# Plain fp32 value matmuls, to-and-fro triples and a packed copy of h in a two-layer encoder step

## The chip, the cores and the metric
The kernel runs on one core of a Trainium2 chip. The time is device microseconds of one execution of the whole program. Five engines work from queues of their own and meet at semaphores: TensorE (PE; its weight loads are shown as PEld), VectorE (DVE), ScalarE (ACT), GpSimd (POOL) and SyncE (SP), which issues most of the DMA transfers.

## What is computed
One inference step of a two-layer encoder on a prompt of 1024 rows and eight samples of 16 rows, 1024 features wide, all in float32. Layer 0 runs differential attention (A, 4 heads of 128) and grouped attention over a sliding window (B, 8 query heads of 64) side by side; layer 1 runs chunk-band attention with a bias by relative position (C, 16 heads of 64). Each attention is followed by a gated feed-forward block with a causal convolution of width 3. Every sub-layer starts with a modulated RMSNorm.

```python
def diff_core(q, k, v, lam, mask):            # A
    s = jnp.einsum('bqhcd,bkhcd->bhcqk', q, k).astype(jnp.float32) * ATTN_SCALE
    p = jax.nn.softmax(jnp.where(mask, s, NEG_INF), axis=-1)
    w = p[:, :, 0] - lam * p[:, :, 1]
    return jnp.einsum('bhqk,bkhe->bqhe', w.astype(v.dtype), v)
...
def relbias_core(q, k, v, table, qpos, kpos, mask):      # C; B likewise, with sinks
    s = jnp.einsum('bqhd,bkhd->bhqk', q, k).astype(jnp.float32) * ATTN_SCALE + bias
    p = jax.nn.softmax(jnp.where(mask, s, NEG_INF), axis=-1)
    o = jnp.einsum('bhqk,bkhd->bqhd', p.astype(v.dtype), v)
...
def conv_ffn(h, conv_state, w_up, conv_w, conv_b, w_down):
    u = h @ w_up
    up = jnp.concatenate([conv_state, u], axis=1)
    y = conv_b
    for j in range(CONV_W):
        y = y + up[:, j:j + t] * conv_w[j]
    a, g = jnp.split(y, 2, axis=-1)
    return (jax.nn.silu(g) * a) @ w_down, up[:, -(CONV_W - 1):]
```

## The kernel before
The program is a chain of stages: setup, attention A and B with the out-projection of layer 0, feed-forward 0, attention C with its out-projection, feed-forward 1, and the final norm. Features stand on the partitions; a row block of the activation h is 128 features by 1152 columns (1024 of the prompt and 8 x 16 of the samples), and there are 8 of them (k = 0 to 7).

Float32 products are made from parts. A value is kept as a high part (type fp32r, which TensorE takes in one pass) and a low part in bf16 (h and hl, w and wl). mm3 (L84) makes one product from a triple of matmuls: high weights by high values (L86), the upper two bytes of the high weights by the low values (L87), and the low weights by the upper two bytes of the high values (L88). The upper two bytes are read in place by `top` (L79), every second two-byte element. pair3 (L114) is the same triple for the values of B and C, with v as the weights and 256 columns of softmax weights (two heads) as the moving operand. mm9 (L90) makes three triples at a time for one weight block of the feed-forward, with the columns of h in pieces of 512, 512 and 128, and puts the three fp32r matmuls (L96) next to each other; L98 is upper weights by hl, L100 low weights by the upper half of h.

Attention goes over tiles: four A tiles (T = 0 to 3), four B tiles, eight C tiles. A tile has eight units u of 128 queries and two stream units for the samples. The steps of a tile are laid out by hand in tile_steps (L1278), and every engine walks through the same list. For unit u the softmax weights E are transposed by TensorE (step T, L1940, L1945, L1950), ACT copies them from PSUM to W as fp32r (L2201), and VectorE subtracts W from the same PSUM bank to get the bf16 low part Wl (L2339). Step V (L1955 on) waits for that subtraction (semaphore w_low) and multiplies W, Wl with v, vl, one triple per block of 128 keys: as many blocks as the unit sees, u + 1 in A, min(u + 1, 2) in B, min(u + 1, 5) in C. v itself is copied by ACT (L2180) and its low part vl made by VectorE (L2328), both in step VS. A stream unit's values (step PV, L1980) are already done in plain fp32 from Ws, in four column tiles of 32. Ws shares its memory with Wl.

Between these steps the planner places the projections as fill: steps F make q, k and v of the next tile, and at the end steps P make the first 6 of 8 parts of the out-projection. Each of them is one mm3 for one k and one third (384) of the columns, and the steps of one third follow each other in the order of k, with the tile's own steps in between. They have due places in the list; a third whose last k is done is evacuated by ACT.

In the feed-forward, first_pair (L896) multiplies the first two up tiles while the norm is still being made, one k at a time: VectorE scales (L628), ACT writes the high part of h (L598, semaphore hp_high), VectorE the low part (L633). The other 42 up tiles run up_tile (L918) with one mm9 per k. GpSimd only loads the convolution state (L845) and makes small copies (L872, L873) in this stage.

Of the kernel before, what the change touches and what calls it, by code (L numbers as in the profile page):

```python
# [8 lines left out]
F32 = mybir.dt.float32  # L9
# [5 lines left out]
P = 128  # L15
# [74 lines left out]
def mm9(pe, ps, acc, w, wl, x, xl, start, stop):  # L90

    def one(b, which, first, last):
# [7 lines left out]
        return pe.matmul(out, wl, top(x[:, lo:hi]), start=first and start, stop=last and stop, skip_group_check=True)  # L100
# [13 lines left out]
def pair3(pe, out, v, vl, w, wl, start, stop):  # L114

    pe.matmul(out, v, w, start=start, stop=False, skip_group_check=True)
    pe.matmul(out, top(v), wl, start=False, stop=False, skip_group_check=True)
    return pe.matmul(out, vl, w.bitcast(BF16)[:, :, 1::2], start=False, stop=stop, skip_group_check=True)
# [585 lines left out]
def ffn(nc, S, G, ins, outs, l):  # L704
    ctx = ExitStack()
    with ctx:
# [19 lines left out]
        ring.own[fb + FCH - 1] = sb("w_z", [P, D], F32R), sb("wl_z", [P, D], BF16)  # L726
        if l == 0:
# [114 lines left out]
        def _(pool):  # L842
# [16 lines left out]
            earlier(0)  # L859

# [31 lines left out]
        def _(pe):  # L892
# [86 lines left out]
            def body(i):  # L979
# [9 lines left out]
                else:  # L989
                    first_pair(c)  # L990
                c += 1
# [385 lines left out]
def attention(nc, S, G, ins, outs, kinds):  # L1377
    ctx = ExitStack()
    with ctx:
# [19 lines left out]
        Ws = Wl[:, :].bitcast(F32)  # L1399
# [438 lines left out]
        def _(pe):  # L1838
# [3 lines left out]
            def do(what, kind, T, s, c, turns):  # L1842
                n = kv(kind, T)
                first = isinstance(T, int) and T == T0
                if what == "F":
# [10 lines left out]
                    mm = mm3(pe, ps[:, f_bank(T, name, b), 0:hi - lo], w[:, k * P:(k + 1) * P], wl[:, k * P:(k + 1) * P],  # L1856
                             h[:, k, lo:hi], hl[:, k, lo:hi], k == 0, k == KT - 1)
# [23 lines left out]
                elif what == "P":  # L1881
# [12 lines left out]
                    mm = mm3(pe, ps[:, i % 2, 0:hi - lo], w[:, k * P:(k + 1) * P], wl[:, k * P:(k + 1) * P],  # L1894
                             h[:, k, lo:hi], hl[:, k, lo:hi], k == 0, k == KT - 3)
# [56 lines left out]
                elif what == "V" and s[1] < QB:  # L1952
# [8 lines left out]
                    for j in range(nb):  # L1961
                        x, y = slice(j * P, (j + 1) * P), slice((k0 + j) * P, (k0 + j + 1) * P)
                        if kind == "A":
                            mm = mm3(pe, ps[:, 7, 0:P], W[:, x], Wl[:, x], v[:, y], vl[:, y], j == 0, j == nb - 1)
                        else:
                            both, low = (t[:, 0:2 * nb * P].rearrange("p (z x) -> p z x", z=2)[:, :, x] for t in (W, Wl))
                            mm = pair3(pe, pair_o(kind, u).rearrange("p (z x) -> p z x", z=2), v[:, y], vl[:, y], both, low,
# [141 lines left out]
        def _(act):  # L2109
# [17 lines left out]
            def do(what, kind, T, s, c, turns):  # L2127
# [49 lines left out]
                elif what == "VS":  # L2177
                    act.wait_ge(S.v_rows, n + 1)
                    act.copy(vn[:, :], sw[:, SEQ:TOK])
                    act.copy(v[:, :], sw[:, :]).then_inc(S.v_high, 1)  # L2180
# [12 lines left out]
                elif what == "T":  # L2193
# [100 lines left out]
        def _(dve):  # L2294
# [16 lines left out]
            def do(what, kind, T, s, c, turns):  # L2311
# [14 lines left out]
                elif what == "VS":  # L2326
                    dve.wait_ge(S.v_high, n + 1)
                    dve.tensor_tensor(vl[:, :], sw[:, :], v[:, :].bitcast(F32), ALU.subtract).then_inc(S.v_low, 1)  # L2328
# [4 lines left out]
                elif what == "T":  # L2333
                    u, p = s[1:]
                    if u >= QB:
                        return
# [357 lines left out]
```

## Time and profile before

| | us |
|---|---|
| median of 3 runs | 3491.92 (3490.02 to 3502.86) |
| the profiled execution | 3502.18 |
| its span on the core | 3500.6 |
| TensorE busy | 3215.5 (92%) |
| VectorE busy | 1853.9 (53%) |
| ACT busy | 1195.0 (34%) |
| GpSimd busy | 428.0 (12%) |

Read the busy time of each engine by stage first, then, for the engine that is busy nearly all the time, what ended its waits, and last single stretches in order of time. Times in the rows are microseconds from the start of the span, unless marked ns.
### The profile page before, as it was taken

How to read it: one execution, taken by the hardware profiler on the slowest of the kernel's cores; microseconds unless marked ns; L12 is line 12 of the kernel's file. 1: busy time of each engine (PE TensorE's matmuls, PEld its weight loads, DVE VectorE, ACT ScalarE, POOL GpSimd, SP SyncE). 2: the span in 40 equal slices, each digit the busy share in tenths (PEclk: the TensorE clock that was granted, in tenths of full speed). 3: DMA queues.
4: the chain of work that ended last, by engine and by line, in shares of the span. 5: the costliest groups of instructions: out<-in, count | busy, mean ns of one | idle time of the engine just before them, and what ended most of it. 6: DMA issues, size and time to landing. Idle time of an engine off the chain costs nothing. (4 is left out here: it accounts for less than half of the span.)

```text
span 3500.6 us, 53118 instructions
## 1 busy us (share of the span) xinstructions
PE 3215.5 (92%) x20564; PEld 2019.7 (58%) x20758; DVE 1853.9 (53%) x3222; ACT 1195.0 (34%) x2527; POOL 428.0 (12%) x820
## 2 busy tenths in 40 slices
PE   7888896888899999999979999998989999999998
PEld 3455553445566666666545555555555666666665
DVE  4355554554655545554555555554636555555546
ACT  3355554533321222222235555554433122222121
POOL 1132222311000000000002222221110000000000
PEclk7899997989999999999999999999999999999998
DMA  9233332231422222222123443444421111111111
GB/s 355 79 105 106 86 90 61 77 115 34 123 62 67 67 66 61 61 79 87 50 84 110 134 133 126 135 135 153 132 64 46 43 49 43 43 43 38 43 43 61
DMA packets 247845, 305.16 MB, mean 87 GB/s; under 512 B 25027, under 2 KB 199607, under 8 KB 247042
## 3 DMA queue, kind: packets, MB, share of 16 engines
q1 hardware_dynamic: 217762, 191.78, 17.5%
q0 software_dynamic: 29920, 111.15, 10.5%
q8 instruction: 109, 1.79, 0.2%
q14 instruction: 54, 0.44, 0.0%
HBM read 265.99 MB, written 64.10 MB: 94 GB/s over the span
## 5 line engine op out<-in xcount | busy, mean ns | idle before, releaser
L96 PE MATMUL psum<-h,ffn_high 128*128 128x512 f32 (+1 forms) x2016 | 587.0, 399 | 2.8 <-ACT u L1069 2.8
L98 PE MATMUL psum<-hl,ffn_high 128*128 128x512 bf16 (+1 forms) x2016 | 553.3, 328 | 0.0
L96 PEld LDWEIGHTS psum<-h,ffn_high 128*128 128x128 f32 x2016 | 377.9, 188 | 134.7 <-issue 8.4
L100 PE MATMUL psum<-h,ffn_low 128*128 128x512 bf16 (+1 forms) x1901 | 444.1, 328 | 7.4
L86 PE MATMUL psum<-h,attC_high 128*128 128x384 f32 (+2 forms) x768 | 361.6, 471 | 23.9 <-issue 8.3
L1142 DVE TENSOR_SCALAR y<-u,cvT 128x1168 f32<-128x1168 f32 x88 | 78.1, 888 | 521.2 <-ACT u L1074 521.0
L86 PE MATMUL psum<-h,attAB_high 128*128 128x384 f32 (+2 forms) x672 | 326.2, 486 | 18.3 <-DVE attAB_low L189 8.5
L98 PEld LDWEIGHTS psum<-hl,ffn_high 128*128 128x128 bf16 x2016 | 194.9, 97 | 244.7
L96 PE MATMUL psum<-actr,ffn_high 128*128 128x512 f32 (+1 forms) x960 | 277.5, 397 | 7.5 <-DVE xT L672 7.5
L98 PE MATMUL psum<-actl,ffn_high 128*128 128x512 bf16 (+1 forms) x960 | 265.0, 330 | 0.0
L1068 ACT COPY u<-psum 128x1024 f32<-128x1024 f32 x88 | 89.3, 1015 | 511.5 <-PE psum L98 511.1
L87 PE MATMUL psum<-hl,attC_high 128*128 128x384 bf16 (+2 forms) x766 | 262.1, 342 | 0.0
L88 PE MATMUL psum<-h,attC_low 128*128 128x384 bf16 (+2 forms) x767 | 258.9, 338 | 0.3 <-issue 0.2
L87 PE MATMUL psum<-hl,attAB_high 128*128 128x384 bf16 (+2 forms) x670 | 235.7, 352 | 0.0
L88 PE MATMUL psum<-h,attAB_low 128*128 128x384 bf16 (+2 forms) x671 | 232.6, 347 | 0.3 <-issue 0.2
L672 DVE SCALAR_TENSOR_TENSOR xT<-psum,mod,xT 128x1024 f32<-128x1024 f32 x176 | 224.8, 1277 | 0.0
L96 PEld LDWEIGHTS psum<-actr,ffn_high 128*128 128x128 f32 x960 | 178.2, 190 | 70.4 <-DVE xT L672 16.5
L100 PE MATMUL psum<-actr,ffn_low 128*128 128x512 bf16 (+1 forms) x900 | 212.9, 330 | 3.8
L872 POOL COPY so<-u 128x2 f32<-128x2 f32 x88 | 17.8, 202 | 1520.2 <-ACT u L1069 1520.2
L86 PEld LDWEIGHTS psum<-h,attC_high 128*128 128x128 f32 x768 | 149.6, 195 | 84.0 <-issue 39.6
L86 PEld LDWEIGHTS psum<-h,attAB_high 128*128 128x128 f32 x672 | 136.4, 203 | 66.4 <-issue 29.9
L183 ACT CAST ffn_high<-ffn_raw 128x1024 fp32r<-128x1024 f32 x42 | 44.2, 1053 | 372.6 <-PE psum L98 372.6
(470 smaller groups left out, 5921.4 us busy)
## 6 DMA issues: line engine op xcount, KB each, us to landing
raws<-in_w_up SPq DMA_DIRECT2D x66, 512.0 KB, 3.9
ada_raw<-in_ada_w SPq DMA_DIRECT2D x24, 1024.0 KB, 9.4
m_raw<-in_ada_w SPq DMA_DIRECT2D x48, 512.0 KB, 7.5
raw_C<-in_cache_c_v POOLq DMA_DIRECT2D x64, 256.0 KB, 4.0
out_ck_s<-in_cache_c_k POOLq DMA_DIRECT2D x8, 1984.0 KB, 8.9
out_cv_s<-in_cache_c_v POOLq DMA_DIRECT2D x8, 1984.0 KB, 15.0
raws<-in_w_in_odd SPq DMA_DIRECT2D x24, 512.0 KB, 12.5
raw_C<-in_cache_c_k POOLq DMA_DIRECT2D x48, 256.0 KB, 5.6
```

Of the source, the lines that this page charges most:

```text
L86: pe.matmul(out, w, x, start=start, stop=False, skip_group_check=True)
L87: pe.matmul(out, top(w), xl, start=False, stop=False, skip_group_check=True)
L88: return pe.matmul(out, wl, top(x), start=False, stop=stop, skip_group_check=True)
L96: return pe.matmul(out, w, x[:, lo:hi], start=first and start, stop=last and stop, skip_group_check=True)
L98: return pe.matmul(out, top(w), xl[:, lo:hi], start=first and start, stop=last and stop, skip_group_check=True)
L100: return pe.matmul(out, wl, top(x[:, lo:hi]), start=first and start, stop=last and stop, skip_group_check=True)
L183: act.copy(self.buffers(c)[0][:, :], self.raw[c % self.raws][:, :]).then_inc(self.high[s], 1)
L672: return dve.scalar_tensor_tensor(out=G.xT[:, n, 0:SEQ], in0=y[:, 0:SEQ], scalar=G.mod[:, a, 16 + n, 0:1], in1=G.xT[:, n, 0:SEQ], op0=ALU. ...
L872: pool.tensor_copy(so[:, 2 * g + j, 0:2], U[g][:, SEQ:SEQ + 2])
L1068: act.copy(U[gate][:, 2:2 + SEQ], ps[:, 3 * gate:3 * gate + 2, :].rearrange("p b n -> p (b n)"))
L1142: ch.then(dve.tensor_scalar(y[:, 0:n], u[:, 2:2 + n], cv[:, l, 2, bass.ds(f, 1)], cv[:, l, 3, bass.ds(f, 1)], ALU.mult, ALU.add))
```

## The change
There are three parts.

1. Values (steps T, V and VS). W and v become plain fp32 tiles. The low parts Wl and vl, VectorE's subtractions for them and the semaphores of the high parts are gone; ACT's copies now release TensorE directly (w_low, v_low). pair3 and the triple of A give way to `plain`: four fp32 matmuls on 32 columns of the weights each, into 32 partitions of the output each. Ws gets memory of its own.
2. Projections (steps F and P). Odd k run their triple in reverse order, so that the fp32r matmul of an odd k is the last of its triple and that of the next even k the first of its own.
3. Feed-forward 1 only. GpSimd copies h to a packed bf16 tile hb, one copy of 128 x 1024 after each hp_high and one of 128 x (8 x 128) for the samples after hs_high, ahead of its other work in the stage. The 42 up tiles read hb in place of the upper half of h (L100). TensorE waits for all nine copies after first_pair.

```diff
+def mm3_to_and_fro(pe, out, w, wl, x, xl, k, stop):
+
+    if k % 2 == 0:
+        return mm3(pe, out, w, wl, x, xl, k == 0, stop)
+    pe.matmul(out, wl, top(x), start=False, stop=False, skip_group_check=True)
+    pe.matmul(out, top(w), xl, start=False, stop=False, skip_group_check=True)
+    return pe.matmul(out, w, x, start=False, stop=stop, skip_group_check=True)
+
+
-def mm9(pe, ps, acc, w, wl, x, xl, start, stop):
+def mm9(pe, ps, acc, w, wl, x, xl, start, stop, xb=None):
...
-        return pe.matmul(out, wl, top(x[:, lo:hi]), start=first and start, stop=last and stop, skip_group_check=True)
+        whole = top(x[:, lo:hi]) if xb is None else xb[:, lo:hi]
+        return pe.matmul(out, wl, whole, start=first and start, stop=last and stop, skip_group_check=True)
...
-def pair3(pe, out, v, vl, w, wl, start, stop):
-
-    pe.matmul(out, v, w, start=start, stop=False, skip_group_check=True)
-    pe.matmul(out, top(v), wl, start=False, stop=False, skip_group_check=True)
-    return pe.matmul(out, vl, w.bitcast(BF16)[:, :, 1::2], start=False, stop=stop, skip_group_check=True)
+def plain(pe, out, w, x, start, stop):
+
+    for j in range(4):
+        cols = slice(32 * j, 32 * j + 32)
+        mm = pe.matmul(out[cols], w[:, cols], x, start=start, stop=stop, skip_group_check=True)
+    return mm
...
+        hb = sb("hb", [P, KT, TOK], BF16) if l else None
...
+            if l:
+                for k in range(KT):
+                    pool.wait_ge(S.hp_high, KT * m + k + 1)
+                    settle(pool, S)
+                    pool.tensor_copy(hb[:, k, 0:SEQ], h[:, k, 0:SEQ].bitcast(F32)).then_inc(S.h_short, 1)
+                pool.wait_ge(S.hs_high, m + 1)
+                settle(pool, S)
+                pool.tensor_copy(hb[:, :, SEQ:TOK], h[:, :, SEQ:TOK].bitcast(F32)).then_inc(S.h_short, 1)
...
-                             h[:, k, :], hl[:, k, :], k == 0, k == KT - 1)
+                             h[:, k, :], hl[:, k, :], k == 0, k == KT - 1, hb[:, k, :] if l else None)
...
                     first_pair(c)
+                    if l:
+                        pe.wait_ge(S.h_short, KT + 1)
...
-        v, vl = sb("v", [P, TOK], F32R), sb("vl", [P, TOK], BF16)
+        v = sb("v", [P, TOK])
...
-        W, Wl = sb("W", [P, 1280], F32R), sb("Wl", [P, 1280], BF16)
+        W, Ws = sb("W", [P, 1280]), sb("Ws", [P, 640])
...
-                            mm = mm3(pe, ps[:, 7, 0:P], W[:, x], Wl[:, x], v[:, y], vl[:, y], j == 0, j == nb - 1)
+                            mm = plain(pe, ps[:, 7, 0:P], W[:, x], v[:, y], j == 0, j == nb - 1)
...
-                    if u < QB:
-                        act.copy(W[:, cols], src).then_inc(S.w_high, 1)
-                    else:
-                        act.copy(Ws[:, cols], src).then_inc(S.w_low, 1)
+                    act.copy((W if u < QB else Ws)[:, cols], src).then_inc(S.w_low, 1)
...
-                elif what == "VS":
-                    dve.wait_ge(S.v_high, n + 1)
-                    dve.tensor_tensor(vl[:, :], sw[:, :], v[:, :].bitcast(F32), ALU.subtract).then_inc(S.v_low, 1)
...
-                    dve.wait_ge(S.w_high, t_no(kind, T, u, p) - 2 * T)
-                    cols, src = probs_at(kind, T, u, p)
-                    dve.tensor_tensor(Wl[:, cols], src, W[:, cols].bitcast(F32), ALU.subtract).then_inc(S.w_low, 1)
```

## Rows read from the trace of the kernel before

**Rows 1.** Stages C and feed-forward 1: stretch, length, busy by engine, clock, DMA share, GB/s

```profile
1764.00:2663.00 899.00, 798.70 (x5740) 504.52 (x5744) 457.81 (x1004) 408.68 (x903) 163.65 (x252) 0.97 0.38 119
2663.00:3472.00 809.00, 798.36 (x4635) 513.75 (x4720) 455.94 (x527) 189.37 (x293) 34.38 (x120) 1.00 0.13 40
```

**Rows 2.** What TensorE waited for, 1831 to 2545 (C): total, times, longest us

```profile
PE psum L116 <- DVE Wl_C L2339: 27.8, 24, 2.3
...
PE psum L1950 <- DVE Wl_C L2339: 7.9, 16, 1.6
```

**Rows 3.** What TensorE waited for, 533 to 832 (B tiles)

```profile
PE psum L1945 <- DVE E_AB L2460: 14.3, 4, 8.4
PE psum L116 <- DVE Wl_AB L2339: 13.6, 15, 1.9
```

**Rows 4.** What TensorE waited for, 93 to 533 (A tiles)

```profile
PE psum L86 <- DVE actl_AB L2351: 8.8, 13, 2.2
```

**Rows 5.** TensorE in order of time, value triples of C: start, us, operation

```profile
2050.85 0.36 PE L116 MATMUL psum<-W_C,v_C 128*128 128x256 f32 x1
...
2051.91 0.36 PE L116 MATMUL psum<-W_C,v_C 128*128 128x256 f32 x1
```

**Rows 6.** TensorE in order of time, a run of column tiles (stream values of C)

```profile
2075.57 0.33 PE L88 MATMUL psum<-h,attC_low 128*128 128x384 bf16 x1
2075.83 1.08 PE L1980 MATMUL psum<-raw_C,Wl_C 128*32 128x128 f32 x32
2076.73 0.40 PE L1980 MATMUL psum<-vn_C,Wl_C 128*32 128x128 f32 x8
...
2077.35 0.34 PE L87 MATMUL psum<-hl,attC_high 128*128 128x384 bf16 x1
```

**Rows 7.** TensorE in order of time, value triples of A

```profile
364.37 0.30 PE L86 MATMUL psum<-v_AB,W_AB 128*128 128x128 f32 x1
...
364.86 0.31 PE L86 MATMUL psum<-v_AB,W_AB 128*128 128x128 f32 x1
```

**Rows 8.** TensorE in order of time, projection triples: the first and the fifth

```profile
2012.17 0.48 PE L86 MATMUL psum<-h,attC_high 128*128 128x384 f32 x1
...
2014.27 0.48 PE L86 MATMUL psum<-h,attC_high 128*128 128x384 f32 x1
```

**Rows 9.** TensorE in order of time, value units that wait: [idle before <-releaser]

```profile
2057.14 0.39 PE L116 MATMUL psum<-W_C,v_C 128*128 128x256 f32 x1 [1.25 <-DVE Wl_C L2339]
...
2062.58 0.38 PE L116 MATMUL psum<-W_C,v_C 128*128 128x256 f32 x1 [1.05 <-DVE Wl_C L2339]
```

**Rows 10.** ACT in order of time, the copy that belongs to the first of them

```profile
2054.88 0.37 ACT L2201 CAST W_C<-psum 128x256 fp32r<-128x256 f32 x1 [0.41 <-PE psum L1950]
```

**Rows 11.** VectorE by line and shape, 1764 to 2663: busy us, mean ns, idle before

```profile
L2339 DVE TENSOR_TENSOR Wl_C<-psum,W_C 128x512 bf16<-128x512 f32 x96 | 62.7, 687 | 115.3 <-ACT W_C L2201 115.3
```

**Rows 12.** TensorE in order of time, two steps of mm9

```profile
2900.02 0.59 PE L98 MATMUL psum<-hl,ffn_high 128*128 128x512 bf16 x2
...
2901.56 0.59 PE L98 MATMUL psum<-hl,ffn_high 128*128 128x512 bf16 x2
```

**Rows 13.** TensorE by line and shape, 2703 to 3440 (feed-forward 1)

```profile
L98 PE MATMUL psum<-hl,ffn_high 128*128 128x512 bf16 x624 | 184.8, 377 | 0.0
L100 PE MATMUL psum<-h,ffn_low 128*128 128x512 bf16 x575 | 179.8, 386 | 3.1
```

**Rows 14.** GpSimd by line and shape, the whole span

```profile
L1668 POOL MEMSET bt_C<- 128x768 f32 x1 | 0.7, 746 | 0.0
```

**Rows 15.** ACT in order of time, the last row block of h

```profile
2651.70 1.15 ACT L598 ACTIVATE h<-u,mod 128x1024 fp32r<-128x1024 f32 x1 [1.36 <-DVE u L628]
```

**Rows 16.** GpSimd and VectorE in order of time, the same microsecond

```profile
2665.26 0.79 POOL L873 COPY so<-u 128x16 f32<-128x16 f32 x1
...
2665.11 0.89 DVE L1142 TENSOR_SCALAR y<-u,cvT 128x1168 f32<-128x1168 f32 x1 [9.81 <-ACT u L1074]
```

**Rows 17.** TensorE in order of time, in first_pair

```profile
2645.38 0.49 PE L86 MATMUL psum<-h,ffn_high 128*128 128x512 f32 x1 [0.45 <-DVE hl L633]
```

More of the change, by code:

```diff
@@ L1398, in attention @@
         Qs, kn, vn = sb("Qs", [P, P]), sb("kn", [P, P]), sb("vn", [P, P])
-        Ws = Wl[:, :].bitcast(F32)
         early = [E[:, e:e + 512].rearrange("p (j d) -> p j d", d=P) for e in ((640, 1920) if odd else (1280,))]
@@ L1855, in do @@
                     lo, hi = THIRDS[b]
-                    mm = mm3(pe, ps[:, f_bank(T, name, b), 0:hi - lo], w[:, k * P:(k + 1) * P], wl[:, k * P:(k + 1) * P],
-                             h[:, k, lo:hi], hl[:, k, lo:hi], k == 0, k == KT - 1)
+                    mm = mm3_to_and_fro(pe, ps[:, f_bank(T, name, b), 0:hi - lo], w[:, k * P:(k + 1) * P],
+                                        wl[:, k * P:(k + 1) * P], h[:, k, lo:hi], hl[:, k, lo:hi], k, k == KT - 1)
                     if k == KT - 1:
@@ L1893, in do @@
                     lo, hi = THIRDS[b]
-                    mm = mm3(pe, ps[:, i % 2, 0:hi - lo], w[:, k * P:(k + 1) * P], wl[:, k * P:(k + 1) * P],
-                             h[:, k, lo:hi], hl[:, k, lo:hi], k == 0, k == KT - 3)
+                    mm = mm3_to_and_fro(pe, ps[:, i % 2, 0:hi - lo], w[:, k * P:(k + 1) * P], wl[:, k * P:(k + 1) * P],
+                                        h[:, k, lo:hi], hl[:, k, lo:hi], k, k == KT - 3)
                     if k == KT - 3:
@@ L1963, in do @@
                         if kind == "A":
-                            mm = mm3(pe, ps[:, 7, 0:P], W[:, x], Wl[:, x], v[:, y], vl[:, y], j == 0, j == nb - 1)
+                            mm = plain(pe, ps[:, 7, 0:P], W[:, x], v[:, y], j == 0, j == nb - 1)
                         else:
-                            both, low = (t[:, 0:2 * nb * P].rearrange("p (z x) -> p z x", z=2)[:, :, x] for t in (W, Wl))
-                            mm = pair3(pe, pair_o(kind, u).rearrange("p (z x) -> p z x", z=2), v[:, y], vl[:, y], both, low,
+                            both = W[:, 0:2 * nb * P].rearrange("p (z x) -> p z x", z=2)[:, :, x]
+                            mm = plain(pe, pair_o(kind, u).rearrange("p (z x) -> p z x", z=2), v[:, y], both,
                                        j == 0, j == nb - 1)
@@ L2179, in do @@
                     act.copy(vn[:, :], sw[:, SEQ:TOK])
-                    act.copy(v[:, :], sw[:, :]).then_inc(S.v_high, 1)
+                    act.copy(v[:, :], sw[:, :]).then_inc(S.v_low, 1)
                 elif what == "KR":
@@ L2332, in do @@
                     maxima(kind, T, s[1], 0, stream_width(kind))
[L2333 to L2336, printed above, removed]
-                    dve.wait_ge(S.w_high, t_no(kind, T, u, p) - 2 * T)
-                    cols, src = probs_at(kind, T, u, p)
-                    dve.tensor_tensor(Wl[:, cols], src, W[:, cols].bitcast(F32), ALU.subtract).then_inc(S.w_low, 1)
                 elif what == "FA":
@@ L2586, in __init__ @@
             "rope_in dup_in qz_zero q_evac k_evac v_evac q_high q_low")
-        (self.k_high, self.k_low, self.v_high, self.v_low, self.v_rows, self.k_rows, self.v_turned, self.k_turned) = make(
-            "k_high k_low v_high v_low v_rows k_rows v_turned k_turned")
+        (self.k_high, self.k_low, self.h_short, self.v_low, self.v_rows, self.k_rows, self.v_turned, self.k_turned) = make(
+            "k_high k_low h_short v_low v_rows k_rows v_turned k_turned")
         (self.stored,) = make(
@@ L2594, in __init__ @@
             "qz scores stream_scores nmax exps probs turned")
-        (self.w_high, self.w_low, self.pv, self.od, self.od_turned, self.squares, self.ms, self.rstd) = make(
-            "w_high w_low pv od od_turned squares ms rstd")
+        (self.w_low, self.pv, self.od, self.od_turned, self.squares, self.ms, self.rstd) = make(
+            "w_low pv od od_turned squares ms rstd")
         (self.o_rows, self.o_turned, self.act_high, self.act_low, self.out_ready, self.out_evac) = make(
```

## The prediction

> **What bounds the kernel now.** The first view to read is the busy time of the engines by stage. In the second feed-forward stage TensorE is busy 798 of 809 us, in attention C 799 of 899 [rows 1]; VectorE is about half busy in both. So in the feed-forward stage a nanosecond taken from a matmul is a nanosecond of the time, while attention C holds some 100 us in which TensorE stands still. The second view says for what: in the steady part of C its largest entry is the low part of the softmax weights, Wl, which VectorE makes at L2339: 27.8 us in 24 waits ahead of the value matmuls and 7.9 in 16 ahead of the next transposes [rows 2]. In the B tiles the same subtraction costs 13.6 us and other work of VectorE 14.3 [rows 3]. In the A tiles no wait names it, but 8.8 us go to actl (L2351), another VectorE step that queues behind it [rows 4]. The change takes that subtraction away and pays with TensorE time, so the two must be set against each other; the two other parts are small and certain by comparison.
>
> **Plain values, the cost.** Per tile and per value unit u (8 per tile, 16 tiles, 128 units) the code runs one block per 128 keys. By the loops these are 1+2+...+8 = 36 blocks per A tile, 1+7x2 = 15 per B tile, 1+2+3+4+5x4 = 30 per C tile.
> A block of B or C is now a triple over 256 columns: four of them take 2050.85 to 2051.91, less the first, so three steps are 1.06, 0.353 each [rows 5]. After it is four 32-column fp32 matmuls. The trace has this form already in the stream values, L1980: 40 records in one run, which are 5 blocks, 4 column tiles, 2 passes [rows 6]. The first 32 records (8 passes over 128 columns) start 0.90 ahead of the last 8, so a pass of the four tiles is 0.1125 at most and two are 0.225; four cycles a column at the granted 2.4 GHz would be 0.213. I take 0.22 for 128 columns and 0.43 for 256. A block of B or C so costs 0.077 more. A block of A is now 0.245 (two from 364.37 to 364.86 [rows 7]) and becomes 0.025 cheaper.
> There is also an edge. Around that run L88 starts at 2075.57 and the next L87 at 2077.35: 1.78. Without it L88 to L87 is 0.36 (a step of 0.525 [rows 8] less one bf16 matmul of 384 columns, 0.16 at 2.4 GHz). Less ten passes (1.10) this leaves 0.32 for entering and leaving the column tiling. That is paid for each of the 128 units, as the triples of before have no edge of that kind.
> Sum: C 8 x (30 x 0.077 + 8 x 0.32) = 39.0; B 4 x (15 x 0.077 + 2.56) = 14.9; A 4 x (2.56 - 36 x 0.025) = 6.6. In all +60.5 us of TensorE time. Bounds: if the exit (a weight load of the next triple, some two thirds of the edge) is hidden, 60 - 27 = 33; with 0.225 and 0.45 per block 68.
>
> **Plain values, the relief.** The release of a unit becomes the end of ACT's copy of W. At 2057.14 TensorE had waited 1.25 for Wl [rows 9], since 2055.89; ACT's copy of that piece had ended at 2055.25 [rows 10]. That wait goes altogether. What is late next is the last unit of a tile, as at 2062.58 (1.05) [rows 9], where I leave 0.47 because ACT's copy itself comes late; the same allowance for the waits at the stage's end leaves 30 of 35.7 us. A wait also costs more than its idle time: from L88's end in the run of matmuls to the first value matmul the pipeline refills, 0.1 to 0.27 us, I take 0.17: 40 x 0.17 = 7. C gains 37 (bounds 20, if 0.7, the length of one subtraction [rows 11], goes from each of the 24 and half of the 16 stays, to 43).
> In B the subtraction follows ACT's copy directly and is 0.7 long [rows 11], so of the 13.6 two thirds go, 9; and VectorE, quit of it, serves its other waits (14.3) earlier: 5 more. B gains 14 (5 to 18). In A the subtraction stands ahead of actl: of 8.8 I take 6, and 3 for the maxima and factors behind it: 9 (0 to 12). The subtractions for vl lie under the projections and are worth nothing. Sum of the relief 60, so plain values net +60.5 - 60 = **+0.5 us**.
>
> **Reversed triples.** A step of four triples of 384 columns is 2.10 from 2012.17 to 2014.27, 0.525 each [rows 8]; 1152 columns at 2.4 GHz are 0.480, so 45 ns go to overhead, in which is one change to fp32 weights and back. A step of mm9 does three times the columns with one such change: 1.540 [rows 12], 100 ns over 1.440. If s is the price of the change and t what goes with the columns, s + t = 45 and s + 3t = 100: t = 27, s = 18. Turned odd k put the fp32 matmul of odd k beside that of k + 1 where the planner leaves the two adjacent, which, counted in the planner's order of steps, is 368 times in 1344 triples (most runs between other steps are two long). 368 x 18 = 6.6 us at most; as the second fp32 weight load has only 0.16 us of matmul to hide under, I take 0.0145: **-5.3**. Bounds: 0.03 lost each time, +11, and -13 if the odd step's end beside fp32 transposes also counts.
>
> **The two-byte copy of h.** L100 reads the upper half of h in place: 386 ns against 377 for L98, which reads packed hl with the same columns [rows 13]; 9 ns. 42 up tiles x 8 k x 2 pieces of 512 x 9 ns = **-6.0** (bounds 0 to -9), all on the path, since this stage is TensorE. The copies: a GpSimd memset of 768 columns is 0.746 [rows 14], so 1024 columns are 1.0 us by estimate, nine of them. The wait on h_short stands behind first_pair. The last h is written by ACT at 2652.85 [rows 15]; copies queued behind it end by some 2656, and TensorE gets there at 2663: 7 us of cover, nothing behind it on TensorE's queue is late. If the copies were three times as long they would still end in time. On GpSimd's own queue only the first state rows (due 2665) stand behind them. But each copy starts on the same event as VectorE's low(k), L633. In the trace a GpSimd copy of 128x16 that is otherwise 0.2 to 0.3 us lasts 0.79 and ends with VectorE's L1142 beside it [rows 16]: the two hold each other up. TensorE waits for low(3) at 2645.38 (0.45 idle) [rows 17], and has growing slack after it. I take **+1.5** (bounds 0 and +4.2).
> The Trainium skill says of this pair of engines (SBUF — State Buffer, section "SBUF: two separate sides") that they share a port pair as an exclusive lock for a whole instruction, and that a VectorE operation with two SBUF inputs takes it against a GpSimd operation that reads SBUF. The trace agrees as far as [rows 16] goes; by that rule every one of the eight low(k) could lose a whole copy, about 8 us by estimate, of which the slack takes half.
>
> **Sum.** +0.5 - 5.3 - 6.0 + 1.5 = -9.3. The profiled execution took 3502.18 (span 3500.6 and 1.6 around it) and would take 3492.9. It was 10.3 above the median of the runs, 3491.92; on the median the forecast is 3482.6, said as 3483. What a measurement of this kernel can tell from no change is about 0.5%, 17.5 us.
>
> **Rivals.**
> Slow: the relief doesn't come. ACT's copies are late too: ACT waits for the transposes (0.41 ahead of its copy [rows 10]) and runs the evacuations in between, so TensorE, arriving at the same place, stops on the copy. With the low bounds C gains 20, B 5, A 0: 25 in place of 60, and the time is 3483 + 35 = 3518. It turns slower than 0.5% when less than 33 of the 60 comes back. Against it: in the row looked at the copy ended 0.6 us ahead of TensorE's need.
> Fast: the edge is mostly hidden. The triple that follows a unit begins with a bf16 weight load where k is odd, and the exit, two thirds of 0.32, is that load; half of the units gain 0.2: -13. VectorE, quit of the subtractions, also takes half of what is left of B's 14.3 and A's waits, and pipeline refills at 0.27: -12. That gives 3458.
> Small parts fail: the strided read is no cost of its own, and the 9 ns come from the place behind fp32 or a weight load (+6); the merged fp32 loads aren't covered, so no gain and a few lost (+8); VectorE is held (+3). Then 3500. The Trainium skill gives a reason for the first (SBUF — State Buffer, the box on cachelines under "Door 1: The DMA port swizzle"): two-byte elements may be strided free as long as two hits fall in a 16-byte line, which every second element does. By it the copy would bring 0 instead of -6.0; the rows show 386 against 377.
> The change doesn't do what it says: if the four column tiles ran one after the other, a block would cost four times 0.43; the 40 records in 1.8 us [rows 6] exclude that.
>
> **How the numbers follow.** Forecast (sum between -25 and +8, own range 3467 to 3500) 0.48, fast 0.20, small parts fail 0.20, slow 0.12. The range runs from 3457 to 3508: it leaves out most of the slow case and less than half of the fast one. Faster by over 0.5% (under 3474.5): the fast case and a fifth of the forecast, 0.30. Slower (above 3509.4): slow case and a little of the third, 0.13. The rest, 0.57, within 0.5%.
>
> **What would show it.** Right: in C no wait on L2339's place longer than 0.6 us but the last unit's, TensorE's busy time in C up by 35 to 45 us at about equal length of the stage; L1980-like runs with 0.32 around them; L86 twice in a row with a step of two triples near 1.03; L100 at L98's 377; first_pair longer by under 4. Wrong: TensorE waits on L2201 in the same number as before on L2339, an edge of 0.1 or of 0.5, or L100 unchanged.

## The result, and the profile after

The changed kernel takes 3457.96 us (median of 4 runs, 3450.08 to 3461.78) beside 3495.13 for the kernel before (median of 4): a ratio of 0.9889 with a 95% interval of 0.9861 to 0.9917. Measured again beside eleven more runs of before it was 0.9876 (0.9861 to 0.9890). So it is faster by 37 to 43 us. The forecast was 3483, a gain of 9.3: the sign was right, and the size a quarter of what came. The time lies a microsecond inside the lower end of the stated range (3457 to 3508), and beside the 3458 of the fast rival, for reasons that neither had.

First the busy time of the engines by stage. The columns are the stretch, its length, busy time and instructions of TensorE, its weight loads, VectorE, ACT and GpSimd, then the granted clock of TensorE, DMA share and GB/s. The four stretches are the A tiles, the B tiles with the out-projection, attention C, and feed-forward 1 from the first up tile on. Kernel before:

```profile
97.40:520.29 422.89, 376.53 (x2757) 240.54 (x2761) 215.46 (x524) 208.05 (x522) 112.26 (x183) 0.95 0.33 94
520.29:889.32 369.03, 289.39 (x1893) 168.88 (x1888) 189.88 (x517) 148.89 (x445) 73.03 (x115) 0.89 0.25 74
1779.77:2633.52 853.75, 763.12 (x5562) 485.61 (x5565) 426.38 (x978) 393.65 (x887) 158.37 (x242) 0.98 0.39 121
2665.03:3494.58 829.55, 815.48 (x4732) 529.11 (x4818) 467.77 (x538) 189.44 (x292) 34.38 (x120) 0.99 0.14 43
```

The same four of the changed kernel:

```profile
94.86:505.02 410.16, 360.98 (x3477) 236.93 (x3481) 187.37 (x472) 207.92 (x522) 112.85 (x183) 0.97 0.34 97
505.02:865.89 360.87, 290.71 (x2195) 166.95 (x2188) 169.09 (x483) 149.29 (x445) 72.52 (x115) 0.90 0.25 75
1755.39:2589.18 833.79, 769.70 (x6765) 477.51 (x6765) 339.58 (x826) 395.35 (x887) 159.62 (x243) 0.99 0.39 124
2621.54:3442.46 820.92, 813.17 (x4818) 530.96 (x4818) 467.77 (x538) 189.51 (x292) 34.94 (x120) 0.99 0.14 43
```

A is 12.7 us shorter, B and its out-projection 8.2, C 20.0, feed-forward 1 8.6. (These two executions are 52 us apart, more than the medians: the one of before was among the longest of its kernel, the one of the changed kernel the shortest.) In C, TensorE is busy 6.6 us longer in a stage 20 us shorter, where the prediction's sign of being right was 35 to 45 us longer at about equal length. And in the three attention stretches the granted clock is a hundredth or two higher. A hundredth of a stretch of 400 us is 4 us, so that column can't be passed over; the experiments below come back to it.

Next what TensorE waited for in steady C of the changed kernel (total, times, longest us):

```profile
PE psum L1966 <- DVE E_C L2468: 10.0, 13, 1.1
...
PE psum L128 <- DVE actl_C L2364: 5.9, 8, 1.1
...
PE psum L1971 <- ACT W_C L2221: 2.0, 3, 1.3
...
PE psum L128 <- ACT W_C L2221: 1.0, 2, 0.5
```

The 35.7 us of [rows 2] are gone. What is late next is not ACT's copy (3.0 in all) but actl, one per tile, 5.9: the last unit of a tile, which the forecast had left at 0.47 for ACT's copy and which waits 0.6 to 1.1 for another step.

One plain value unit of four blocks, TensorE in order of time, with plain values alone:

```profile
2019.78 0.33 PE L88 MATMUL psum<-h,attC_low 128*128 128x384 bf16 x1
2020.04 1.93 PE L124 MATMUL psum<-W_C,v_C 128*32 128x256 f32 x32
2021.91 0.55 PE L1956 MATMUL psum<-consts,E_C 128*128 128x128 f32 x3
```

and the same unit in the kernel before, first and last of its rows:

```profile
2035.17 0.33 PE L88 MATMUL psum<-h,attC_low 128*128 128x384 bf16 x1
...
2036.77 0.49 PE L1950 MATMUL psum<-consts,E_C 128*128 128x128 f32 x3
```

From L88 to the transposes it was 1.60 and is 2.13: 0.53 dearer, where the forecast had 4 x 0.077 + 0.32 = 0.63 with an exit that partly falls behind the transposes. The prices of [rows 5, 6] carry over: in the trace of plain values with the subtraction still waited for (below), units of C that don't wait are dearer by 0.30, 0.38, 0.45, 0.53 and 0.61 with one to five blocks, which is 0.077 a block, as forecast, and an edge of 0.22 before what falls behind.

### The profile page after: what moved, and what is told of

It is laid out like the page before. It is cut to its first block and busy times, and to the rows that moved or that the text cites. A ratio compares the mean times of both kernels' runs of the same rounds, so it can differ in the third digit from the quotient of the medians.

```text
span 3448.5 us, 57532 instructions
## 1 busy us (share of the span) xinstructions
PE 3210.5 (93%) x22978; PEld 2005.8 (58%) x22978; DVE 1719.6 (50%) x2984; ACT 1197.2 (35%) x2527; POOL 442.6 (13%) x829
## 3 DMA queue, kind: packets, MB, share of 16 engines
q8 instruction: 126, 2.06, 0.3%
## 5 line engine op out<-in xcount | busy, mean ns | idle before, releaser
L110 PE MATMUL psum<-h,ffn_low 128*128 128x512 bf16 (+1 forms) x1008 | 225.8, 332 | 0.0
L110 PE MATMUL psum<-hb,ffn_low 128*128 128x512 bf16 (+1 forms) x1008 | 219.5, 327 | 0.0
L86 PE MATMUL psum<-h,attC_high 128*128 128x384 f32 (+2 forms) x408 | 159.7, 394 | 21.3 <-issue 8.3
L96 PE MATMUL psum<-h,attC_high 128*128 128x384 f32 x360 | 170.1, 473 | 0.0
L86 PE MATMUL psum<-h,attAB_high 128*128 128x384 f32 (+2 forms) x360 | 148.1, 412 | 17.8 <-DVE attAB_low L200 8.5
L107 PEld LDWEIGHTS psum<-actl,ffn_high 128*128 128x128 bf16 x960 | 93.2, 97 | 117.4 <-issue 2.5
L96 PE MATMUL psum<-h,attAB_high 128*128 128x384 f32 x312 | 150.5, 482 | 0.0
L87 PE MATMUL psum<-hl,attC_high 128*128 128x384 bf16 (+2 forms) x408 | 138.8, 340 | 0.0
L88 PE MATMUL psum<-h,attC_low 128*128 128x384 bf16 (+2 forms) x408 | 136.7, 335 | 0.0
```

Source lines behind the costliest of these rows:

```text
L86: pe.matmul(out, w, x, start=start, stop=False, skip_group_check=True)
L87: pe.matmul(out, top(w), xl, start=False, stop=False, skip_group_check=True)
L88: return pe.matmul(out, wl, top(x), start=False, stop=stop, skip_group_check=True)
L96: return pe.matmul(out, w, x, start=False, stop=stop, skip_group_check=True)
L107: return pe.matmul(out, top(w), xl[:, lo:hi], start=first and start, stop=last and stop, skip_group_check=True)
L110: return pe.matmul(out, wl, whole, start=first and start, stop=last and stop, skip_group_check=True)
```

## The experiments

All times stand beside runs of the kernel before on the same chip. Besides the ratio I read one more number from the runs. Each run lists its span and its mean granted clock; the clock has two levels in these traces, 1.0 (2.4 GHz) and 0.5. Span times clock is the time the span would have at full clock, and the rest is lost to stretches at the half clock (an upper bound, since a TensorE that stands loses nothing; but in the profiles TensorE is at half clock for 250 us before and 198 after, and busy for 197 and 149 of these, so nearly all of the fall is time in which it works). Before: 3372 and 122 us, the mean of 23 runs. Differences are to before, with two standard errors; the clock is listed to a thousandth.

### Plain values alone
The edit leaves out the other two parts:

```diff
-    if k % 2 == 0:
-        return mm3(pe, out, w, wl, x, xl, k == 0, stop)
...
+    return mm3(pe, out, w, wl, x, xl, k == 0, stop)
...
-                    if l:
-                        pe.wait_ge(S.h_short, KT + 1)
```

> Plain fp32 values alone; the triples of the projections all forward, the low-weight matmuls of feed-forward 1 read h in place. Theory W (what the change gains is TensorE's standing still for Wl, and the half-clock stretches that go with it): 20 to 30 us below the kernel before, two thirds of the gain of the whole change, in attention AB and C alike, with fewer microseconds at the granted clock 0.5 in both. Rival R (the gain is the reversed triples): within 6 us of before. The forecast's sum said +0.5.

3477.44 beside 3495.44, ratio 0.9939 (0.9922 to 0.9955), spans shorter by 18.8 in the mean. At full clock that is only -4.5 ± 1.6; -14.3 ± 4.1 is less time lost to the half clock. So plain values alone give about half of the gain, a little under the 20 to 30 us and two thirds of theory W, and three quarters of what they gave came through the clock. The forecast's +0.5 answers to the -4.5, and had nothing for the rest.

### Reversed triples alone

```diff
-                    mm = mm3(pe, ps[:, f_bank(T, name, b), 0:hi - lo], w[:, k * P:(k + 1) * P], wl[:, k * P:(k + 1) * P],
+                    mm = mm3_to_and_fro(pe, ps[:, f_bank(T, name, b), 0:hi - lo], w[:, k * P:(k + 1) * P],
```

> To-and-fro triples alone, values as before. Theory W: 6 to 14 us below the kernel before, at most a third of the gain. Rival R (odd k ends with an fp32 matmul, so that the fp32 transposes, scores or values behind a run of projections start earlier, 0.1 us in each of 451 runs): 25 to 40 us below, and plain values alone do little. The forecast's sum said -5.3.

3492.36 beside 3495.44, 0.9986 (0.9973 to 0.9999): -4.8 in the mean of the spans, -6.1 ± 2.8 at full clock and no change in the lost part (+1.3 ± 5.1). Rival R falls, W's 6 to 14 us was a little too much as well, and the forecast had -5.3.

### The packed copy alone

```diff
+        whole = top(x[:, lo:hi]) if xb is None else xb[:, lo:hi]
...
+                    pool.tensor_copy(hb[:, k, 0:SEQ], h[:, k, 0:SEQ].bitcast(F32)).then_inc(S.h_short, 1)
...
+                    if l:
+                        pe.wait_ge(S.h_short, KT + 1)
```

> The packed copy of h in feed-forward 1 alone. The forecast's sum said -6.0 + 1.5 = -4.5, of which -6 to -9 lie between the first up tile and the last down tile and 0.5 to 2 are lost in first_pair. Rival (strided two-byte reads are free): the stage of the up tiles as long as before, the whole 0 to +2.

3490.1 beside 3495.44, 0.9981 (0.9970 to 0.9993); at full clock -8.2 ± 2.0. The step of mm9 shows it, here in the changed kernel, TensorE in order of time:

```profile
2855.68 0.87 PE L105 MATMUL psum<-h,ffn_high 128*128 128x512 f32 x3
...
2857.20 0.87 PE L105 MATMUL psum<-h,ffn_high 128*128 128x512 f32 x3
...
2858.71 0.87 PE L105 MATMUL psum<-h,ffn_high 128*128 128x512 f32 x3
```

Two steps take 3.03, 1.515 each, where [rows 12] have 1.54. Over the whole stage the median step is 1.513 in each kernel with the copy and 1.540 in each without: 27 ns for each of 336 steps, 9 us, and not the 18 ns that the two pieces of 512 gave. The rival of the free strided read, and with it the rule that spoke against this part, doesn't hold here. In first_pair the copies meet VectorE's work. GpSimd and then VectorE in the changed kernel, and last a step of VectorE in the kernel before:

```profile
2598.33 1.04 POOL L876 CAST hb<-h 128x1024 bf16<-128x1024 f32 x1 [3.74 <-ACT h L609]
2600.84 1.88 POOL L876 CAST hb<-h 128x1024 bf16<-128x1024 f32 x1 [1.47 <-ACT h L609]
...
2600.54 1.28 DVE L644 SCALAR_TENSOR_TENSOR hl<-u,mod,h 128x1024 bf16<-128x1024 f32 x1
...
2588.95 2.06 DVE L200 TENSOR_TENSOR ffn_low<-raws,ffn_high 128x1024 bf16<-128x1024 f32 x1
```

```profile
2633.29 1.22 DVE L189 TENSOR_TENSOR ffn_low<-raws,ffn_high 128x1024 bf16<-128x1024 f32 x1
```

A copy by itself takes 1.04, as estimated. The second begins 0.3 after L644 and takes 1.88, until 0.90 after the end of L644 at 2601.82: nearly a whole copy behind it. L644 keeps its 1.28. So the two do exclude each other, as the Trainium skill has it (SBUF — State Buffer, section "SBUF: two separate sides"), and at the low parts of h it is GpSimd that waits, and it has time. That was to be read in [rows 16] too: VectorE's L1142 takes 0.88 to 0.91 in all 88 of its places, so there only GpSimd was held up, not each by the other. The other way round it happened at a step that the forecast did not look at. L200, the low part of a weight tile (L189 before), meets the first copy and takes 2.06 in place of 1.22, and every later step of VectorE in first_pair begins 0.84 later. That is nearly the whole price: first_pair takes 32.33 to 32.36 us in the profiles with the copy and 31.48 to 31.51 in those without, 0.85 more, within the bounds and below the 1.5 taken. The 9 us less this 0.85 are the 8.2 measured.

### Whole values
One matmul for a block in place of four column tiles, on the changed kernel:

```diff
-    for j in range(4):
-        cols = slice(32 * j, 32 * j + 32)
-        mm = pe.matmul(out[cols], w[:, cols], x, start=start, stop=stop, skip_group_check=True)
-    return mm
+    return pe.matmul(out, w, x, start=start, stop=stop, skip_group_check=True)
```

> The changed kernel with each block's values as one fp32 matmul on all 128 columns of the weights in place of four column tiles of 32. If the edge of column tiling (about 0.2 to 0.3 us on each of 128 units) is a price that the tiling alone brings, this is 15 to 30 us below the changed kernel. Rival: a full-width plain fp32 weight load is not hidden under a block's matmul as the loads of the tiles are, 0.1 us or more on each of 444 blocks, and it is 20 us or more above the changed kernel.

3445.14, ratio 0.9841 (0.9822 to 0.9859), some 13 us below the changed kernel, just short of the 15 to 30. In the profiles five steady tiles of C are 9.7 us shorter (428.3 from the first value matmul of the first tile to that of the sixth, against 438.0) and the A tiles 5.1 longer (415.24 against 410.16). The edge was a price of the tiling alone, as the forecast had assumed it. The unit of four blocks in C, from the kernel with whole values for B and C further down, which has the same whole matmuls there:

```profile
2005.87 0.33 PE L88 MATMUL psum<-h,attC_low 128*128 128x384 bf16 x1
2006.04 1.89 PE L126 MATMUL psum<-W_C,v_C 128*128 128x256 f32 x8
2007.77 0.49 PE L1976 MATMUL psum<-consts,E_C 128*128 128x128 f32 x3
```

1.90 where the tiles took 2.13: 0.23, and 0.06 more behind it, where eight transposes take 0.79 in place of 0.85.

### The subtraction kept, and waited for
Plain values alone, with the old low part still made and still waited for:

```diff
-                    act.copy((W if u < QB else Ws)[:, cols], src).then_inc(S.w_low, 1)
+                    if u < QB:
+                        act.copy(W[:, cols], src).then_inc(S.w_high, 1)
...
+                    dve.wait_ge(S.w_high, t_no(kind, T, u, p) - 2 * T)
+                    dve.tensor_tensor(Wl[:, cols], src, W[:, cols], ALU.subtract).then_inc(S.w_low, 1)
```

> Plain fp32 values alone, but VectorE still makes the low part of W from the same PSUM bank and TensorE still waits for it (nobody reads it). What is left of the change is TensorE's own work. If the forecast's cost is right (a block of B or C 0.077 us dearer, 0.32 us of edge per unit, +60 us in all), it is 35 to 60 us above the kernel before. If the edge and the blocks are cheaper than that, as the pace in steady C suggests (idle time down by 15 us at equal length), it is 5 to 25 us above. In both cases the difference to plain values alone is what the missing wait and the freed VectorE bring.

3515.71 beside 3498.44, 1.0055 (1.0037 to 1.0072). At full clock +29.3 ± 3.1, and the lost time changes by -9.5 ± 6.0. So TensorE's own work is dearer by less than half of the forecast's +60.5. The traces show where. Taken from the operation before each value unit to the one behind it, away from the half clock, the units of C are dearer by 24.8 us (61 of 64 units; 39.0 forecast), those of B by 3.1 (28 of 32; 14.9 forecast) and those of A by nothing (-0.4, 30 of 32; 6.6 forecast). Two things make the difference. A unit that begins after a wait has paid its entry before: a C unit of five blocks is 0.61 dearer without a wait and 0.41 with one, which is little more than its blocks. And added work that stands ahead of a wait shortens it: in C the waits for the subtraction fall from 35.7 to 29.4 us. More than half of the units of A and nearly half of those of B begin after a wait.

### The subtraction kept, and not waited for

```diff
+                    dve.wait_ge(S.w_low, t_no(kind, T, u, p))
+                    x = G.consts[:, 0:P].unsqueeze(1).broadcast_to([P, nb, P])
+                    dve.tensor_tensor(idle[:, 0:nb * P].rearrange("p (n d) -> p n d", d=P), x, x, ALU.subtract).then_inc(S.idled, 1)
```

> Plain fp32 values alone, and VectorE still does a subtraction of the same size at the same place, on constants, for which nobody waits. If the gain is the shorter path from transposes to values, this is within 5 us of plain values alone (3472 to 3482). If it is VectorE's freed time (actl, factors and maxima behind the subtraction come earlier), half of the gain or more is lost: 3483 to 3495.

3505.32 beside 3498.44, 1.0022 (1.0011 to 1.0032); at full clock +19.1 ± 2.3. That is above both expectations. Read as it stands, of the 33.8 us at full clock between the waited subtraction and none at all the shorter path to the values brings 10 and VectorE's freed queue 24. But the stand-in is dearer than the original. It also waits for the one before it, and where a unit has two pieces in A it holds VectorE 1.20 where the original holds it 1.01. The A tiles show it, first with the subtraction that is waited for, then with the stand-in that nobody waits for:

```profile
95.60:517.35 421.75, 370.22 (x3477) 232.13 (x3481) 209.92 (x520) 208.18 (x522) 113.43 (x183) 0.96 0.33 94
95.33:523.66 428.33, 370.18 (x3478) 232.76 (x3482) 211.60 (x520) 207.96 (x522) 113.37 (x183) 0.96 0.33 93
```

A wait less can't by itself make them 6.6 us longer, so at least that much of the 24 belongs to the stand-in, and path and queue come out about equal, some 17 each; how they divide more exactly stays open. By place it is plainer: C takes 875 us with the wait, 854 with the stand-in and 846 with no subtraction, so there the path is the larger part; the A tiles gain only when the subtraction itself goes, to 413. TensorE, VectorE and ACT at one unit, with the stand-in:

```profile
390.00 0.85 PE L124 MATMUL psum<-v_AB,W_AB 128*32 128x128 f32 x16 [2.42 <-DVE actl_AB L2356]
...
388.24 1.35 DVE L2344 TENSOR_TENSOR idle_AB<-consts 128x512 bf16<-128x512 f32 x2 [2.24 <-ACT W_AB L2207]
389.51 0.34 DVE L2356 SCALAR_TENSOR_TENSOR actl_AB<-psum,columns,actr_AB 128x128 bf16<-128x128 f32 x1
...
387.64 0.94 ACT L2207 COPY W_AB<-psum 128x512 f32<-128x512 f32 x2
```

and with no subtraction:

```profile
380.74 0.71 PE L124 MATMUL psum<-v_AB,W_AB 128*32 128x128 f32 x17 [0.17 <-DVE actl_AB L2344]
...
380.24 0.35 DVE L2344 SCALAR_TENSOR_TENSOR actl_AB<-psum,columns,actr_AB 128x128 bf16<-128x128 f32 x1 [2.88 <-ACT actr_AB L2239]
```

The values of a unit wait until actl has left their PSUM bank. With the stand-in in the queue, VectorE stands at it until ACT has copied W, does two pieces, and only then comes to actl: TensorE waits 2.42. Without it actl goes as soon as its own input is there, and TensorE waits 0.17. The wait's name (actl) says nothing of the subtraction; its place in the queue does.

### Whole values for B and C, tiles for A

```diff
-                            mm = plain(pe, pair_o(kind, u).rearrange("p (z x) -> p z x", z=2), v[:, y], both,
+                            mm = whole(pe, pair_o(kind, u).rearrange("p (z x) -> p z x", z=2), v[:, y], both,
```

> The changed kernel with whole 128-column matmuls for the value blocks of B and C (256 columns each) and column tiles of 32 for A (128 columns). With whole matmuls everywhere the A tiles were 5 us longer and B, C 16 us shorter in the profiles. If a whole weight load hides under 256 columns and not under 128, this is 3 to 7 us below whole matmuls everywhere, some 3438 to 3442. If the 5 us in A were the clock (25.6 against 22.2 us at half clock), it is the same as that, 3445.

3438.85, ratio 0.9833 (0.9820 to 0.9847): the fastest kernel here, but not told apart from whole values everywhere (0.9841) by the ratios. At full clock it is -39.4 ± 2.8 against -37.0 ± 2.7. The A tiles are 410.7 in its profile against 415.2.

### The changed kernel again, and without the copy

The first is the changed kernel itself; the second lacks the copy of h:

```diff
-                             h[:, k, :], hl[:, k, :], k == 0, k == KT - 1, hb[:, k, :] if l else None)
+                             h[:, k, :], hl[:, k, :], k == 0, k == KT - 1)
```

> The changed kernel once more, beside the two kernels below on one chip. Span times mean granted clock is read as its time at full clock, the rest of the span as lost to the half clock. From the runs so far: 22 us less at full clock than the kernel before and 17 us less lost, 0.988 to 0.990 of before. If the first four runs were a lucky draw of the clock, the second part shrinks and the ratio is 0.991 to 0.994.

> Plain values and to-and-fro triples without the packed copy. If the parts add up, at full clock 10 us less than before (4.5 and 6) and 13 to 16 us less lost to the half clock, 24 to 27 us in all. If the reversed triples bring more behind plain values than alone (run ends in fp32 beside fp32 values), 15 us or more less at full clock.

The changed kernel: 3453.23 beside 3496.59, -23.1 ± 3.8 at full clock and -20.1 ± 4.9 lost. The gain through the clock was no draw. Without the copy 3464.99, 0.9912 (0.9898 to 0.9927): -15.5 ± 2.9 and -16.3 ± 4.0. So step by step, at full clock: plain values -4.5, the reversed triples on top of them -11.0, the copy on top -7.6. Behind plain values the reversed triples bring more than alone (-6.1), though the two differ by hardly more than their errors. The traces bear both out. The planner leaves 451 runs of triples, the same in every kernel; from the operation before a run to the one behind it, away from the half clock, the runs are 5.6 us shorter with the reversal alone (426 runs) and 9.0 behind plain values (429).

Inside a run, two triples that meet with their fp32r matmuls take a step of 1.028 in place of 1.047: 19 ns for each of 380 such places, close to the forecast's 18 (it took 14.5). The ends of a run count too. A pair that starts forward and ends on its fp32r matmul ahead of transposes gains about as much, 0.02. A reversed pair behind the bf16 matmuls of the scores gains 0.11. Plain values alone, TensorE in order of time:

```profile
1830.12 0.39 PE L2080 MATMUL psum<-k_C,ql_C 64*128 64x512 bf16 x2
1830.44 0.45 PE L86 MATMUL psum<-h,attC_high 128*128 128x384 f32 x1
...
1831.69 0.85 PE L124 MATMUL psum<-W_C,v_C 128*32 128x256 f32 x12
```

and with the reversed triples on top:

```profile
1825.85 0.39 PE L2084 MATMUL psum<-k_C,ql_C 64*128 64x512 bf16 x2
1826.17 0.34 PE L94 MATMUL psum<-h,attC_low 128*128 128x384 bf16 x1
...
1827.31 0.85 PE L128 MATMUL psum<-W_C,v_C 128*32 128x256 f32 x12
```

From the scores to the values it was 1.57 and is 1.46. The other kind is what makes the reversal worth less alone. Before, and with the reversal alone:

```profile
1842.43 0.45 PE L86 MATMUL psum<-h,attC_high 128*128 128x384 f32 x1
...
1843.45 0.42 PE L116 MATMUL psum<-W_C,v_C 128*128 128x256 f32 x1
```

```profile
1824.22 0.44 PE L86 MATMUL psum<-h,attC_high 128*128 128x384 f32 x1
...
1825.35 0.28 PE L125 MATMUL psum<-W_C,v_C 128*128 128x256 f32 x1
```

The pair that ends on its fp32r matmul ahead of a value triple, which begins with one, takes 1.13 in place of 1.02: 0.12 lost, in the median of 16 such pairs. Ahead of plain values the same pairs gain 0.02. That is some 2 us of the difference.

One place misleads. In the kernel before, a pair ahead of two transposes takes 1.30:

```profile
2053.14 0.42 PE L86 MATMUL psum<-h,attC_high 128*128 128x384 f32 x1
...
2054.44 0.41 PE L1950 MATMUL psum<-consts,E_C 128*128 128x128 f32 x2
...
2053.60 1.29 DVE L2339 TENSOR_TENSOR Wl_C<-psum,W_C 128x512 bf16<-128x512 f32 x2 [1.71 <-ACT W_C L2201]
```

With plain values alone, the triples still all forward, it is 1.14:

```profile
2037.63 0.42 PE L86 MATMUL psum<-h,attC_high 128*128 128x384 f32 x1
...
2038.77 0.38 PE L1956 MATMUL psum<-consts,E_C 128*128 128x128 f32 x2
```

and in the changed kernel 1.12. So 0.16 of it is the subtraction: its first half ends at 2054.29 and the transposes begin 0.15 later; at the neighbouring places where the profile does list their wait for it, they begin 0.14 after its end. It doesn't appear as idle time here, since the modelled end of the L88 before it covers it. Only 0.02 is the reversal.

### The first matmul of a unit repeated
A try at the clock: more TensorE work in the kernel before, with nothing else changed.

```diff
+                            for _ in range(2):
+                                pe.matmul(dst, first_w, first_x, start=True, stop=False, skip_group_check=True)
```

> The kernel before with the first fp32r matmul of each of the 128 value units issued three times in place of once (a start overwrites, so the result is the same). That is 32 x 2 x 0.053 us in A, 32 x 2 x 0.107 in B, 64 x 2 x 0.107 in C, 24 us more TensorE work at full clock, with every wait left as it is; what a wait follows on it shortens. Theory (a busier TensorE keeps its clock): the share lost to the half clock falls by 5 to 12 us, as it did with plain values and the wait left in, and the span grows by 8 to 19. Rival (the clock rises because the stops for VectorE get shorter): nothing changes in the lost share, span +16 to +24.

3513.47 beside 3496.59, 1.0045 (1.0033 to 1.0057): +20.0 ± 4.0 at full clock, -4.0 ± 5.7 lost. Neither theory is decided by that. The work costs nearly its face value; the lost part falls by less than the theory wanted and may not fall at all.

## Why the forecast was wrong in size, point by point

Three steps of the prediction failed. Its sum had no term for the half clock, which gave 14 to 20 us. Its cost and its relief of plain values, 60.5 and 60, were each about twice what came at full clock, 29 and 34. And its price of the reversed triples, -5.3, counted only the merged pairs inside a run, where -11 came. The copy's term was right in kind and short by some 3 us.

**The sum had no term for the clock.** Every price was taken at 2.4 GHz. The time lost to the half clock falls by 14 to 20 us in each measurement with plain values and no subtraction, by 9.5 and 11.4 with the subtraction kept, and by nothing that can be measured with triples (reversed or not, with the copy or not). That is the largest single part of the missing 28 to 34 us. The single profiles show the place. In the A tiles TensorE is at half clock for 36 to 46 us in the four kernels with value triples and for 22 to 29 in the six with plain values and no subtraction; in C for 34 to 39 and for 11 to 27. The stretch with the lowest clock, B with its out-projection (0.89), keeps it (0.90). That the A tiles lose time so was to be seen in the profile of before. What it looks like in the kernel before, in a stretch of 7 us and the one behind it in the A tiles:

```profile
383.00:390.00 7.00, 6.28 (x23) 3.79 (x24) 3.35 (x11) 3.44 (x7) 1.16 (x3) 0.53 0.01 2
390.00:397.00 7.00, 6.25 (x50) 4.61 (x49) 5.83 (x13) 3.28 (x10) 2.07 (x3) 0.98 0.10 25
```

TensorE is as busy in both by the table, with 23 matmuls in the one and 50 in the other. In the A tiles such stretches add up to 43.7 us in the profile of before and to 22.2 after (but to 36.3 in the copy's profile, which has the same A tiles as before, so part of this fall is the draw). Why the plain values keep the clock stays open: fewer and shorter stops, or the fp32 work itself. The kernel with all waits left in and the one with the repeated matmul lie between, and their errors overlap.

**Plain values, the cost: right per unit, too large in sum.** Block and edge are as priced (0.53 against 0.63 for a unit of four, and the edge vanishes with whole matmuls). But 60.5 us counted every unit as if TensorE had run into it without a stop. Kept behind its waits, the arithmetic cost 29 at full clock: 25 us of it in the units of C, 3 in B and none in A.

**The relief: right in kind, too large by as much.** 60 us were forecast, 33.8 at full clock came back. In A the reason was right: actl stands behind the subtraction. In C the waits on Wl went, as said, and the end of a tile waits for actl instead. The allowance of 0.17 us per wait for a refill was not tested by itself.

So cost and relief were each twice too large and their difference, +0.5, is near the measured -4.5. That nearness is luck: two errors that cancel, in part of the same origin, as the same waits that held the relief also hid part of the cost.

**Reversed triples**: -5.3 forecast, -6.1 alone, -11.0 behind plain values. The merged pairs were priced rightly (19 ns measured, 14.5 taken; 380 counted in the trace against 368). The step that failed is that only these were counted: a run's ends count as well. A reversed pair behind the scores brings 0.11, and a pair that ends on its fp32r matmul ahead of a value triple costs 0.12, which the reversal alone pays and the changed kernel doesn't. The good bound, -13, named only the end beside fp32 transposes, which brings 0.02.

**The copy of h**: -4.5 net forecast, -8.2 alone and -7.6 on top. The term for the strided read was taken from the mean durations of the 512-column pieces alone; the step from start to start held 27 ns where those gave 18. The +1.5 for the collision was 0.85, and at a weight's low part (L189), not at low(k); its reading of [rows 16], that the two engines hold each other up, was wrong there.

**The rivals.** The fast case had the right sign and size (3458), but by other mechanisms than happened: its cheaper exit isn't seen (the whole edge is 0.28 to 0.29 where 0.32 was taken, and it was the wait ahead of a unit that hid it, not the load behind), the refills were not tested, VectorE's other waits fell only in part, and the clock, which made the size, wasn't in it. The slow case didn't occur; ACT's copies come in time (3.0 us of waits in steady C, 5.4 in the B tiles).

## What to carry to other kernels

Work out the time at full clock and the time lost to the half clock separately, for each kernel and over all its runs; a change to a stage that runs below full clock can move the second more than the first. An operation's price in an in-order queue is also what stands behind it there: here the freed place of a VectorE subtraction was worth about as much as the shorter path to the matmul that waited for it. A step from start to start can hold a wait that shows no idle time, so compare it in a kernel without the wait before giving it to something else. And here a column tiling that filled the whole array with one tile width cost its edges for nothing, where the plain matmul with 256 columns kept the same pace.

## What the runs showed of the hardware that was not expected

A plain fp32 matmul on 128 x 128 weights and 256 columns takes the same time as four column tiles of 32 (0.43 us from block to block in both), without the edge of 0.29 us per run (0.23 and 0.06, above); with 128 columns it is dearer by a little, six blocks from the first to the next operation 1.51 against 1.45:

```profile
280.54 1.58 PE L126 MATMUL psum<-v_AB,W_AB 128*128 128x128 f32 x12 [0.97 <-DVE actl_AB L2356]
282.05 0.50 PE L2046 MATMUL psum<-k_AB,q_AB 64*128 64x512 f32 x1
```

```profile
278.73 1.52 PE L124 MATMUL psum<-v_AB,W_AB 128*32 128x128 f32 x48 [0.95 <-DVE actl_AB L2344]
280.18 0.50 PE L2034 MATMUL psum<-k_AB,q_AB 64*128 64x512 f32 x1
```

(the first with whole values, the second with plain values alone). And the spread of one kernel between its executions goes largely with the clock: in 23 runs of the kernel before the spans vary by 5.1 us (standard deviation) and the spans times clock by 3.0. Of the first four runs of the changed kernel the fastest, 3450.08, had a mean granted clock of 0.971, the slowest, 3461.78, of 0.968; three thousandths of the span are 10.4 of these 11.7 us.
